# Two transformer blocks on one core: weight splits, differences, gates and turned copies issued in another order

## The reference, cut to what matters

```python
# first mixer: forgetting attention (8 heads), short conv, HGRN2, joined
y = rms(concat([y_a, y_c, y_r]) by heads) * gain;  y[last] *= silu(r_g);  x = x + y @ w_out
# second mixer
y_a = gqa_axial(...)                       # 8 heads
y_b = softmax(q1 k1) - lam * softmax(q2 k2), times v   # "diff", 8 heads, two softmaxes each
y_c = mla(rms(c_q), rms(c_kv), ...)        # latent attention, 8 heads
x = x + (sum_n sigmoid(gate_n) * (y_n @ w_branch[n])) @ w_out
```

## Time and profile before

| | |
|---|---|
| median of 3 runs | 2555.1 us (2554.83 to 2555.97) |
| the profiled execution's own time | 2549.77 us |
| its span in the profile | 2548.0 us |
| PE busy | 2498.7 us |
| DVE busy | 1885.1 us |
| ACT busy | 1495.8 us |
| mean granted TensorE clock | 0.996 |

### The profile page before, as it was taken

The page is one execution under the profiler, slowest core; times in us unless marked ns, Lnnn a source line. Parts: engine busy times, 40 slices in busy tenths (PEclk is TensorE's granted clock), DMA queues, the critical chain, the costliest instruction groups (busy, mean ns, idle before and its releaser), DMA issues.

```text
span 2548.0 us, 38641 instructions
## 1 busy us (share of the span) xinstructions
PE 2498.7 (98%) x16734; PEld 2231.6 (88%) x16734; DVE 1885.1 (74%) x1665; ACT 1495.8 (59%) x1520; POOL 0.2 (0%) x4
## 2 busy tenths in 40 slices
PE   9999999999999999999999999999999999999998
PEld 8889999877888888888888887998899999899998
DVE  7765556858888888888888888657775575777655
ACT  6463336457777777777777777446553455565433
POOL 0000000000000000000000000000000000000000
PEclk9999999999999999999999999999999999999999
DMA  6335554325999999999999998433345553243552
GB/s 247 133 116 183 182 183 148 133 84 190 364 358 362 359 363 355 363 349 367 352 364 357 364 356 313 173 132 116 133 166 188 178 180 133 101 162 122 188 190 83
DMA packets 83520, 585.38 MB, mean 230 GB/s; under 512 B 9420, under 2 KB 11308, under 8 KB 12820
## 3 DMA queue, kind: packets, MB, share of 16 engines
q1 hardware_dynamic: 83348, 582.87, 61.8%
HBM read 581.79 MB, written 1.05 MB: 229 GB/s over the span
## 4 chain that ended last, share of the span: by engine, by line
PE 88%; DVE 7%; ACT 3%; issue 1%; DMA 0%; DVEq 0%; ACTq 0%
PE PS L1798 87%; DVE wlo L1053 2%; ACT whi L555 1%; PE PS L2331 1%; PE PS L2012 1%; ACT pb L667 1%; DVE stat L1200 1%; DVE pb L1214 1%; DVE hT L1099 0%; ACT pt L684 0%; DVE xT L1378 0%; DVE hlo L1105 0%; DVE pb L1218 0%; DVE hlo L1069 0%; DMA raw<-in_ws 0%
## 5 line engine op out<-in xcount | busy, mean ns | idle before, releaser
L1053 DVE TENSOR_TENSOR wlo<-raw,whi 128x2048 fp32r<-128x2048 f32 x550 | 1257.9, 2290 | 361.7 <-ACT whi L555 352.9
L555 ACT ACTIVATE whi<-raw 128x2048 fp32r<-128x2048 f32 x550 | 1052.0, 1914 | 310.3 <-PE PS L1798 273.4
L1798 PE MATMUL PS<-hhi,whi 128*128 128x256 f32 x1984 | 573.1, 289 | 10.0 <-DVE hlo L1105 2.6
L1798 PE MATMUL PS<-hlo,whi 128*128 128x256 f32 x1984 | 562.4, 283 | 0.0
L1798 PE MATMUL PS<-hhi,wlo 128*128 128x256 f32 x1984 | 562.2, 283 | 0.0
L1798 PEld LDWEIGHTS PS<-hhi,whi 128*128 128x128 f32 x1984 | 381.3, 192 | 24.5 <-issue 16.3
L1798 PEld LDWEIGHTS PS<-hlo,whi 128*128 128x128 f32 x1984 | 381.4, 192 | 0.7 <-issue 0.5
L1798 PEld LDWEIGHTS PS<-hhi,wlo 128*128 128x128 f32 x1984 | 381.3, 192 | 0.0
L1798 PE MATMUL PS<-whi,xghi 128*128 128x512 f32 x896 | 359.9, 402 | 1.2 <-DVE wlo L1053 1.1
L1798 PE MATMUL PS<-whi,xglo 128*128 128x512 f32 x896 | 355.0, 396 | 0.0
L1798 PE MATMUL PS<-wlo,xghi 128*128 128x512 f32 x896 | 354.9, 396 | 0.0
(11 more groups left out here) (374 smaller groups left out, 3574.8 us busy)
## 6 DMA issues: line engine op xcount, KB each, us to landing
raw<-in_wm SPq DMA_DIRECT2D x336, 1024.0 KB, 5.6
raw<-in_ws SPq DMA_DIRECT2D x214, 1024.0 KB, 4.8
xT<-in_xT SPq DMA_DIRECT2D x4, 256.0 KB, 6.8
bsum<-in_bsum SPq DMA_DIRECT2D x1, 1024.0 KB
out_T<-hT SPq DMA_DIRECT2D x4, 256.0 KB, 2.5
lmask<-in_lmask SPq DMA_DIRECT2D x1, 512.0 KB
onehot_in<-in_onehot SPq DMA_DIRECT2D x1, 288.0 KB
lbw<-in_lbw SPq DMA_DIRECT2D x1, 256.0 KB
```

The source lines that it names most:

```text
L555: act.activation(whi[s % SPLIT][:], raw[s % RAW][:], ACT.Copy).then_inc(hi_ready, 1)
L1053: dve.tensor_tensor(wlo[s % SPLIT][:], raw[s % RAW][:], whi[s % SPLIT][:].bitcast(F32), ALU.subtract).then_inc(lo_ready, 1)
L1798: return pe.matmul(out, a, b, start=start, stop=stop, skip_group_check=True)
```

## The change

On all engines together:

- second mixer, start: ACT does both weight splits before `root`, DVE does the next unit's split before it scales bank 4;
- `head_spread` and `head_apply` of the two five-tile head norms use a third bank (`SUMS` = 6 for qa, 3 for cc);
- the first fill after the axial attention goes to bank 4 in place of 7 (the line that filled down to 15 is taken out);
- attention on DVE: the addition of a pair's second part moves from the end of step n to behind the row maximum of step n+1; in the diff attention the DVE's share of a fill moves from even to odd steps (`fill_at=1`); gates of the latent halves move from behind the scaling to ahead of it; `early` (the split of the first latent output half) comes at n = 4 in place of n = 5;
- attention on ACT: in fox the inverse root of step 2 moves behind the copies of the turned probabilities;
- fox on DVE: `head_rest` moves from the end of step 2 to step 3 ahead of the scaling, `head_apply` with the y gate from ahead of the scaling to behind it; the weight splits of step 3 (DVE) and step 4 (ACT) move behind the attention;
- fox on PE: `keep_warm(1, 8)` behind `head_spread` at step 3, that is eight products in each first mixer; `out_half_begun` at step 5 in place of 4, and `out_half_ended` behind the next head sums in place of step 5;
- second mixer, latent: ACT's take stands ahead of the copy that spreads the rotated key (`kc`), in place of behind it.

```diff
# ACT
 def fill(n=1, bank=7): ... out_of(bank, f.dst, f.scale, f.func, f.wide)
 def ahead(n):
...
+    if n == 2:
+        head_inverse_root(7, 16, 1.0 / HD)      # was amid(n == 2)
 def behind(n):
-    if n == 3:
+    if n == 4:
         after(hn_applied); split_y(2); after(hn_applied); after(y_gated); split_y(3)
-    if n == 4:
-        take()
...
 head_square(yT[:, 0:4, :], hT[:, 0:4, :])
+take()
 def second_mixer(l):
     take()
+    take()
     root(0)
-    take()
...
+    fill(len(fillers))
+    take()
     after(rope_done)
     act.activation(kc[NOPE:QW, :, :], ...)
-    fill(len(fillers))
-    take()
# DVE
+if 1 <= n <= len(jobs) and jobs[n - 1].less is not None:
+    first, second = pbs[(n - 2) % PB], pbs[(n - 1) % PB]
+    dve.scalar_tensor_tensor(out=first[:], in0=second[:], scalar=jobs[n - 1].less, in1=first[:], ...)
-if n % fill_every == 0:
+if n % fill_every == fill_at:
     fill()
-if early and n > len(jobs):
+if early and n == len(jobs):
     early()
+if n < len(halves): ... gate(*halves[n], 7)     # was behind the scaling of job n
 def second_mixer(l):
...
+    used_next = take()
     dve.wait_ge(unit_used, used)
     scaled(4, pair(qa, 0)).then_inc(rows_taken, 1)
-    used = take()
-    dve.wait_ge(unit_used, used)
+    dve.wait_ge(unit_used, used_next)
-    head_norm(qa, 5, 16, ..., [4, 5])
+    head_norm(qa, 5, 16, ..., [4, 5, SUMS])
-    attention(diff_heads(), pb2, fill_every=2)
+    attention(diff_heads(), pb2, fill_every=2, fill_at=1)
-    head_norm(cc, 5, 16, gains, [4, 5])
+    head_norm(cc, 5, 16, gains, [4, 5, 3])
# PE, first mixer
     if n == 3:
         head_spread(4, lambda t: selT[:, 4 + t, :], 16, [7, 0])
...
+        claim(1)
+        keep_warm(1, 8)
-    if n == 4:
+    if n == 5:
         held.extend(out_half_begun(4, 0, yhi, ylo))
-    if n == 5:
-        out_half_ended(*held, 4, 0, yhi, ylo)
 attention(fox_heads(l), ...)
 head_sums(4, lambda t: selw[:, t, :], 16, hT[:, 0:4, :], SUMS)
+out_half_ended(*held, 4, 0, yhi, ylo)
# PE, second mixer
-fill(max(0, len(fillers) - 15))
-fill()
+fill(1, 4)
```

More of the change, by code:

```diff
@@ L608, in out_of, with fill @@
                 C.next(drained)
-            def fill(n=1):
+            def fill(n=1, bank=7):
                 for _ in range(min(n, len(fillers))):
                     f = fillers.pop(0)
-                    out_of(7, f.dst, f.scale, f.func, f.wide)
+                    out_of(bank, f.dst, f.scale, f.func, f.wide)
             def split_ahead():
@@ L647, in head_norm, with attention @@
                 fill()
-            def attention(jobs, pbs, pts, fill_every=1, halves=(), early=None, amid=None, ahead=None, behind=None):
+            def attention(jobs, pbs, pts, fill_every=1, halves=(), early=None, ahead=None, behind=None):
                 turned_before, mixed_before = C.now(turned), C.now(mixed)
@@ L669, in attention @@
                         ins.then_inc(exped, 1)
-                    if amid:
-                        amid(n)
                     if n >= 2 and jobs[n - 2].value:
@@ L745, in split_y @@
                     act.activation(yhi[:, 2 * j:2 * j + 2, :], yT[:, 2 * j:2 * j + 2, :], ACT.Copy).then_inc(y_hi, 1)
-                def amid(n):
-                    if n == 2:
-                        head_inverse_root(7, 16, 1.0 / HD)
                 def ahead(n):
@@ L765, in behind @@
                         split_y(3)
-                    if n == 4:
-                        take()
-                attention(fox_heads(l), pb1, pt1, amid=amid, ahead=ahead, behind=behind)
+                attention(fox_heads(l), pb1, pt1, ahead=ahead, behind=behind)
                 act.wait_ge(mixed_out, C.now(mixed_out))
                 head_square(yT[:, 0:4, :], hT[:, 0:4, :])
+                take()
                 head_inverse_root(SUMS, 16, 1.0 / HD)
@@ L1188, in gate, with attention @@
                     C.next(merged)
-            def attention(jobs, pbs, fill_every=1, halves=(), early=None, amid=None, behind=None):
+            def attention(jobs, pbs, fill_every=1, fill_at=0, halves=(), early=None, amid=None, behind=None):
                 turned_before = C.now(turned)
@@ L1201, in attention @@
                                           negate=True).then_inc(max_ready, 1)
-                    if n % fill_every == 0:
+                    if 1 <= n <= len(jobs) and jobs[n - 1].less is not None:
+                        first, second = pbs[(n - 2) % PB], pbs[(n - 1) % PB]
+                        dve.scalar_tensor_tensor(out=first[:], in0=second[:], scalar=jobs[n - 1].less, in1=first[:],
+                                                 op0=ALU.mult, op1=ALU.add).then_inc(probs_ready, 1)
+                        C.next(probs_ready)
+                    if n % fill_every == fill_at:
                         fill()
@@ L1209, in attention @@
                         amid(n)
+                    if n < len(halves):
+                        if halves[n][2]:
+                            dve.wait_ge(unit_used, used)
+                        else:
+                            after(half_done)
+                        gate(*halves[n], 7)
                     if n < len(jobs):
@@ L1216, in attention @@
                             step(ins)
[L1217 to L1225, removed]
-                            dve.wait_ge(unit_used, used)
-                        else:
-                            after(half_done)
-                        gate(*halves[n], 7)
+                        else:
+                            ins.then_inc(probs_ready, 1)
+                            C.next(probs_ready)
+                            if j.value is None:
+                                dve.wait_ge(probs_ready, C.now(probs_ready))
                     if behind:
@@ L1347, in amid, with behind @@
                     if n == 3:
+                        head_rest(16)
+                def behind(n):
+                    if n == 1:
+                        dve.wait_ge(drained, C.now(drained))
+                        dve.scalar_tensor_tensor(out=flat(rgs), in0=flat(rq), scalar=1.0, in1=flat(rgs), op0=ALU.add,
+                                                 op1=ALU.mult).then_inc(gate_made, 1)
+                    if n == 3:
                         head_apply(yT[:, 4:8, :], 4, lambda t: g[:, 4 + t:5 + t], [7, 0])
@@ L1352, in amid @@
                                                  op0=ALU.mult, op1=ALU.mult).then_inc(y_gated, 1)
-                def behind(n):
-                    if n == 1:
-                        dve.wait_ge(drained, C.now(drained))
-                        dve.scalar_tensor_tensor(out=flat(rgs), in0=flat(rq), scalar=1.0, in1=flat(rgs), op0=ALU.add,
-                                                 op1=ALU.mult).then_inc(gate_made, 1)
-                    if n == 2:
-                        head_rest(16)
-                    if n == 3:
                         split_y(2)
                         split_y(3)
-                        take()
                 attention(fox_heads(l), pb1, amid=amid, behind=behind)
+                take()
                 head_rest(16)
@@ L1669, in second_mixer @@
                 step(dve.tensor_scalar(nlam[:, 3:4], vec2(l, "aq"), HD ** -0.5, None, ALU.mult))
-                head_norm(qa, 5, 16, lambda t: nlam[:, 3:4] if t < 4 else vec2(l, "ak"), [4, 5])
+                head_norm(qa, 5, 16, lambda t: nlam[:, 3:4] if t < 4 else vec2(l, "ak"), [4, 5, SUMS])
                 if l == 0:
@@ L1856, in unit_tok, with fill @@
                 ins.then_inc(unit_used, 1)
-            def fill(n=1):
+            def fill(n=1, bank=7):
                 for _ in range(min(n, len(fillers))):
-                    project((unit_tok if fillers.pop(0).tokens else unit_T), 7)
+                    project((unit_tok if fillers.pop(0).tokens else unit_T), bank)
             def project(unit, bank, first=False):
@@ L2439, in second_mixer @@
                 fillers.extend(waiting_projections2())
-                head_norm(5, lambda t: selw[:, t, :], lambda t: selT[:, t, :], 16, hT, [4, 5])
+                head_norm(5, lambda t: selw[:, t, :], lambda t: selT[:, t, :], 16, hT, [4, 5, SUMS])
                 qa_done = C.now(hn_applied)
@@ L2468, in second_mixer @@
                 fill(max(0, len(fillers) - 12))
-                head_norm(5, lambda t: tables["selC"][:, t, :], lambda t: selCT[:, t, :], 16, hT, [4, 5])
+                head_norm(5, lambda t: tables["selC"][:, t, :], lambda t: selCT[:, t, :], 16, hT, [4, 5, 3])
                 fill(len(fillers))
```

1 line of the change is left out of this document (removed).

## The result

The kernel after takes 2535.6 us (median of 4 runs, 2532.23 to 2537.15). The kernel before, run beside it, takes 2554.97 (2554.37 to 2555.97). The ratio is 0.9929, 95% interval 0.9916 to 0.9942: 19.4 us less, where 11.0 were predicted, and outside the predicted range.

The account below looks back on a forecast made before the run. PE, busy 98% of the span, was taken to bound the kernel through its stream order and holes. Wait terms of 9.5 plus 1.5 of clock gave 11.0 us off 2555.1, so 2544.1 us, range 2540.0 to 2551.0.

Parts of the forecast that it names:

- the sum: Both layers: gains from shortened PE waits, part by part, less the fox attention loss, 9.5 us off before any clock gain.
- the clock, 1.5: Three slow stretches of PE's granted clock: one of three counted as gone, 1.5 us off.
- Rival A: All three slow clock stretches go, as their triggers are the removed waits: 14.1 us off, 2541.0; chance 0.17.
- The fox term, -0.6: Fox attention, both layers: new waits and added constant products outweigh the waits removed, a loss of 0.6 us.
- B: Reordering in fox and diff attention only moves the waits, diff gives only 1.0: 5.1 us off, 2550.0; chance 0.10.
- C: Fox and diff waits only move; bank and root waits return one step later: 2 to 3 off, 2552.6; chance 0.13.
- D: Every new short wait starts a slow clock stretch of 1.5 us, making the kernel slower: 2560.6; chance 0.05.

Follow-up runs that it names:

- the kernel after again: The changed kernel, unchanged, run once more beside the others on one chip: 2532.1 us against 2551.8 for the kernel before, ratio 0.9921.
- the rest: Kernel before with only root splits, bank 4 for a fill, latent gates and `early`, and the kc copy changed: 2542.71 us against 2551.8, ratio 0.9966.

## Why the prediction was right in direction and wrong in size

**The waits, by place.** Each forecast row came as laid out: L626, L1138, L1649 and L1179 gone, L1105 near 0.7, L684 at 4.9, the new waits at 1.3 and 0.6, fox attention 0.5 longer. In the two profiled executions the second mixers together are 17.2 us shorter; 4.6 of it are the three low stretches, 12.6 are waits. Ahead of them the kernel after is 2.5 later: 0.5 by fox attention, 1.4 in the experts, and 0.5 by the longer low stretch near 1590. The 1.4 are not the clock, which is at 1.00 there (PE waits 0.45 for DVE at 755, which before does not), and not the change: in the profile of the kernel after again that part is 0.8 shorter than in before. So the order is worth some 12 us in the profiles, where the sum said 9.5.

**The term that was mis-sized first: what a wait is worth.** I priced a removed wait at its idle time. That idle time counts from the modelled end of the last product (0.28 long), while products of this kind start 0.12 apart. The timeline of before ahead of the fifth tile's spread, then that of after at the same place:

```profile
1626.46 0.28 PE L1798 MATMUL PS<-rs_lo,selT 16*128 16x256 f32 x1
1627.23 0.38 PE L1798 MATMUL PS<-rs_hi,selT 16*128 16x256 f32 x1 [0.50 <-DVE qa L1138]
```

```profile
1628.09 0.28 PE L1793 MATMUL PS<-rs_lo,selT 16*128 16x256 f32 x1
1628.21 0.27 PE L1793 MATMUL PS<-rs_hi,selT 16*128 16x256 f32 x1
```

From start to start 0.77 became 0.12: 0.65 for a wait of 0.50, and 0.76 from the first head sum to the turn of `qa` (10.33 to 9.57 in each layer). So this wait returned 0.15 to 0.26 more than its row. By the wait lists some ten went, net of the new ones; if each is taken at that surplus, an estimate, it is 1.5 to 2.6 us in all. That closes the gap between 9.5 and 12.

**The term that failed: the clock, 1.5.** The sentence was "I count one of three as gone: 1.5", beside "I take the difference between the kernels to be the same in both". Both were wrong, in one way: they took one execution for the usual one. The profiled execution of before had a mean clock of 0.996 and no low stretch in fox attention; its usual execution has 0.9945. In the kernel after the mean is 0.9982, 3.7 thousandths or 5.6 to 9.3 us. With 12 of waits that gives 18 to 21, and 19.4 were measured. How the 19.4 divide between the two is an estimate; no run has one without the other. Rival A (all three stretches gone) was right for the profiled pair, whose difference was 14.7 against its 14.1, but its number is luck in part: the waits gave 2.6 more than its sum had, and the 1.9 lost in the experts and near 1590 took most of that back. It too started from that one execution.

**The fox term, -0.6.** Right for the order, and wrong for the time: alone the part gave 3.0, with a clock 2.2 thousandths higher: its waits of 3.65 per layer have low stretches behind them, in 9 of 14 places with the order of before and in none of 10 with the new one. I had argued from their absence in one trace ("no stretch of low clock in its place").

**The parts and the whole.** Alone they gave 2.8, 2.7, 9.1 and 3.0, 17.6 together; the whole gave 19.4 and 19.7. Each has an interval of 2.3 to 2.9 us to either side, so no interaction is shown. That the rest gave 9.1 for 6.1 stays partly open: its waits by the corrected price and its clock at 1.5 give about 9, but the runs spread over 12 us.

**The rivals.** B and C have no support: no wait came back one step later. D was wrong in its count, but its mechanism is there: in the profile of the kernel after the new short waits have clock 1.00 behind them (rows of 1720 and 2185), yet in two of the six traces with the new wait of 1.34 the clock fell behind it in one layer, for 3.4 us of clock each time. The change removed more such waits than it made. So the Trainium skill's rule on short idles (the section named above), which I held up against the change, spoke more for it than against it.

## What to carry to other kernels

On an engine that is 98% busy, a wait of 0.5 to 1.5 us near small products may cost twice: its own time, and at times a low stretch of the clock behind it that no wait shows. Before a sum is set against a median, look at the mean granted clock of all executions, not only of the profiled one; here a single profile stood 5 us off. A removed wait is worth the change from start to start, not its idle time, and filling a wait with constant products pays only where they fall into the wait: a fill that must first wait for its own bank comes on top.

## What was not expected of the hardware

- The number of low stretches differs from execution to execution of one kernel, while the places recur: the first profile of before had them at 1628, 2199 and 2259 (beside one near 1590), the second at 140, 540, 1590, 1630, 1730, 1790 and 2105. Over the 86 executions the span goes from 2547.3 to 2556.2, the shorter the higher the mean clock.
- Added products made the kernel 2.9 us faster, with no other edit.
